# Gate products issued ahead of a block border, and a projection tile cast ahead of the value norm

## What is computed

```python
y_a = chunked_spatial_gating(u, vv, a_spatial_w, a_spatial_b) * silu(a_z)   # vv = layer_norm(gelu(a_v))
gates = sigmoid(g.reshape(bn, s, 3, D_MODEL) + gate_b)                       # g is a slice of h @ w_in
merged = (gates[:, :, 0] * (y_a @ proj_a)
          + gates[:, :, 1] * (y_b @ proj_b)
          + gates[:, :, 2] * (y_m @ proj_m))
x = x + merged @ w_out
```

## Time and profile before

| what | value |
|---|---|
| median of timed runs | 1764.21 us |
| profiled execution | 1767.3 us |
| its span, first to last instruction | 1765.6 us |
| PE busy | 1727.1 us (98%) |
| DVE, ACT, POOL busy | 52%, 37%, 14% |
| mean granted TensorE clock | 0.995 |

### The profile page before, as it was taken

How to read it: one execution, slowest core, us unless ns; L and a number is a source line. 1 busy time by engine, 2 the same in 40 slices (tenths; PEclk the granted TensorE clock), 3 DMA queues, 4 the chain that set the end, 5 groups by cost and what they waited for, 6 DMA issues and landing times.

```text
span 1765.6 us, 22322 instructions
## 1 busy us (share of the span) xinstructions
PE 1727.1 (98%) x8731; PEld 1398.5 (79%) x8731; DVE 915.1 (52%) x1528; ACT 653.4 (37%) x1225; POOL 247.0 (14%) x412
## 2 busy tenths in 40 slices
PE   7999999999999999999999999999999999999998
PEld 5788887778888887778888788888787777777786
DVE  5158868664326753763223322467142555657764
ACT  5234338512324432852112111323213363434731
POOL 3012210288801100000000000490000000000000
PEclk9999999999999999999999999999999999999999
DMA  4121110346232200311111211333613111001132
GB/s 144 55 71 48 36 36 2 118 148 194 77 122 72 60 25 13 93 30 48 54 54 40 84 45 30 108 131 99 129 36 99 37 37 37 25 25 48 38 131 107
DMA packets 148340, 122.93 MB, mean 70 GB/s; under 512 B 10556, under 2 KB 133899, under 8 KB 147595
## 3 DMA queue, kind: packets, MB, share of 16 engines
q1 hardware_dynamic: 148234, 121.49, 22.8%
HBM read 108.21 MB, written 13.26 MB: 69 GB/s over the span
## 4 chain that ended last, share of the span: by engine, by line
PE 53%; DVE 3%; ACT 1%; issue 1%; DMA 1%; SPq 0%; DVEq 0%; ACTq 0%
PE psum L93 29%; PE psum L278 8%; PE psum L81 7%; PE psum L2707 2%; PE psum L2738 2%; PE psum L2721 1%; PE psum L1720 1%; DMA w_raw<-w_in 1%; PE psum L945 0%; PE psum L931 0%; DVE h2T L2340 0%; PE psum L2503 0%; PE psum L2524 0%; PE psum L920 0%; SPq L196 0%
## 5 line engine op out<-in xcount | busy, mean ns | idle before, releaser
L93 PE MATMUL psum<-hT,w_parts 128*128 128x512 f32 x3360 | 796.7, 393 | 7.1 <-PEq L61 3.4
L93 PEld LDWEIGHTS psum<-hT,w_parts 128*128 128x128 f32 x3360 | 629.6, 189 | 144.9 <-issue 9.0
L221 DVE TENSOR_TENSOR w_parts<-w_raw,w_parts 128x1024 fp32r<-128x1024 f32 x88 | 111.6, 1268 | 371.4 <-ACT w_parts L210 371.4
L93 PE MATMUL psum<-h2T,w_parts 128*128 128x512 f32 x1248 | 298.9, 396 | 2.9 <-ACT ssm_u L330 2.9
L93 PEld LDWEIGHTS psum<-h2T,w_parts 128*128 128x128 f32 x1248 | 231.9, 189 | 52.0 <-issue 5.0
L1514 ACT ACTIVATE gate<-psum,cols 128x512 f32<-128x512 f32 x48 | 33.0, 688 | 283.7 <-PE psum L81 283.7
L81 PE MATMUL psum<-y_high,wp_parts 128*128 128x512 f32 x384 | 128.8, 395 | 0.3 <-DVE ya_low L1572 0.3
L210 ACT CAST w_parts<-w_raw 128x1024 fp32r<-128x1024 f32 x88 | 91.6, 1041 | 33.9 <-DMA w_raw<-w_in 29.2
L81 PEld LDWEIGHTS psum<-y_high,wp_parts 128*128 128x128 f32 x384 | 72.0, 188 | 18.9 <-DVE ya_low L1572 1.6
L278 PE MATMUL psum<-w_parts,y_parts 128*128 128x512 f32 x360 | 82.6, 390 | 0.6 <-DVE w_parts L271 0.6
L403 DVE RECIPROCAL x<-x 128x512 f32<-128x512 f32 x24 | 80.3, 3344 | 0.0
(11 more groups left out here) (377 smaller groups left out, 2267.7 us busy)
## 6 DMA issues: line engine op xcount, KB each, us to landing
w_raw<-w_in SPq DMA_DIRECT2D x188, 256.0 KB, 3.4
middle_a<-ada_w SPq DMA_DIRECT2D x32, 384.0 KB, 3.6
w_raw<-w_out SPq DMA_DIRECT2D x16, 512.0 KB, 3.9
qkT<-x SPq DMA_DIRECT2D x8, 512.0 KB, 7.8
w_raw<-m_w_kv SPq DMA_DIRECT2D x16, 256.0 KB, 3.1
base<-x SPq DMA_DIRECT2D x8, 512.0 KB, 4.1
x_kept<-x_ring SPq DMA_DIRECT2D x8, 512.0 KB, 3.4
base<-x_kept SPq DMA_DIRECT2D x8, 512.0 KB, 3.6
```

The costliest lines, as they stand in the source:

```text
L93: last = pe.matmul(out, lhs(a, k), rhs(b, k), start=(n == 0), stop=(n == len(SLOT) - 1))
L221: dve.tensor_tensor(self.parts[:, u, LO, :, :], self.raw[:, :, :], self.parts[:, u, HI, :, :].bitcast(F32), ALU.subtract).then_inc(self.lo ...
```

## The change

TensorE: the 24 products of slot 0 of the merge run are issued by the middle run, 16 ahead of the last turn and 8 behind it, in `FirstProducts`. The merge run then starts with the products of slot 1, and behind them come the projection of slot 0, then that of slot 1. ScalarE and VectorE: the high and the low part of the first gate tile are made when the second last tile of the middle run is done, not at its end. ScalarE, VectorE and SP: the second projection tile is loaded (behind the first tile's low part) ahead of the norm's three loads, cast as soon as slot 1 is done and ahead of the second square root and Gelu, and split ahead of the norm's last steps; `work` now comes ahead of `spatial` in the list.

```diff
@@ Dense.tensor
-            if slot.h == 0:
+            if slot.h == 0 and not (s == 0 and self.opened):
                 pe.wait_ge(self.w.high, 2 * slot.n + 2)
...
+            if s == 0 and self.opened:
+                continue
             slot_part(pe, out, lhs, rhs, range(8))
...
+            if s == 1 and self.opened:
+                tile.extra(pe, self, 0).then_inc(self.made, 1)
+                for work in self.beside:
+                    work.tensor(pe, 0)
             (tile.extra(pe, self, s) or last).then_inc(self.made, 1)
@@ Dense.scalar (Dense.vector likewise with ahead_low)
+            if slot.last and slot.n + 2 == len(self.tiles) and self.ahead:
+                self.ahead.ahead_high(act)
...
-        if self.ahead:
-            self.ahead.ahead_high(act)
+class FirstProducts(Beside):
+    def tensor_end(self, pe):
+        if 0 in self.steps:
+            pe.wait_ge(self.w.high, 2)
+            pe.wait_ge(self.run.free[0], sum(1 for slot in self.run.slots if slot.bank == 0))
+        else:
+            pe.wait_ge(self.w.low, 2)
+        slot_part(pe, bank(self.core, 0, 1), self.w.lhs(0), lambda part, k: self.src[:, part, k, 0:HALF], self.steps)
@@ Projections.sync
-        if s == 0:
+        if s == -1:
             self.load(sp, 1)
@@ Projections.scalar_early
+        if s == 1:
+            act.wait_ge(self.run.made, 2)
+            self.wp_split_high(act, 1)
@@ Projections.vector_early
+        if s == 1:
+            self.wp_split_low(dve, 1)
@@ Projections.scalar (and .vector)
-        if s % 2 and s // 2 + 1 < len(self.tiles):
+        if s % 2 and s // 2 + 1 < len(self.tiles) and s > 1:
@@ merge_run
-    run = Dense(core, w, hT, tiles, [spatial, work])
+    run = Dense(core, w, hT, tiles, [work, spatial])
+    run.opened, work.run = True, run
@@ Middle.prepare
-                               [dilated, self.join, modulation, ssm, mem, turn_mv, attention, self.turn_av],
+                               [dilated, self.join, modulation, ssm, mem, turn_mv, attention, products[0], self.turn_av,
+                                products[1]],
```

More of the change, by code:

```diff
@@ L424, in __init__ @@
     def __init__(self, core, w, src, tiles, beside=(), heads=None, eps=None, ahead=None, crossed=False):
-        self.ahead = ahead
+        self.ahead, self.opened = ahead, False
         self.core, self.w, self.src, self.tiles, self.beside, self.eps = core, w, src, tiles, beside, eps
@@ L554, in vector @@
                 w.split_low(dve, slot.n // 2 + 1, slot.n % 2)
+            if slot.last and slot.n + 2 == len(self.tiles) and self.ahead:
+                self.ahead.ahead_low(dve)
             self.tiles[slot.n].vector(dve, self, s)
@@ L560, in vector @@
         self.tiles[slot.n].vector_last(dve, self, s)
-        if self.ahead:
-            self.ahead.ahead_low(dve)
         for work in self.beside:
@@ L1446, in scalar, with __init__, follow @@
                 act.copy(self.mv[:, t, :], bank(self.core, 6 + t, 1)).then_inc(self.kept, 1)
+class FirstProducts(Beside):
+    def __init__(self, core, w, src, steps):
+        self.core, self.w, self.src, self.steps = core, w, src, steps
+    def follow(self, run):
+        self.run = run
+    def tensor_end(self, pe):
[5 more added lines that the diff above has]
+        slot_part(pe, bank(self.core, 0, 1), self.w.lhs(0), lambda part, k: self.src[:, part, k, 0:HALF], self.steps)
 class TurnTokens(Beside):
@@ L3433, in prepare @@
                               [core.over("mem_pT", [P, 1024], c_at + 8192)[:, :]], (2,), 4, (6,))
+        products = [FirstProducts(core, ahead, self.hT, steps) for steps in (range(16), range(16, 24))]
         self.run = run = Dense(core, w, self.hT, self.tiles,
-                               [dilated, self.join, modulation, ssm, mem, turn_mv, attention, self.turn_av],
+                               [dilated, self.join, modulation, ssm, mem, turn_mv, attention, products[0], self.turn_av,
+                                products[1]],
                                heads=(self.ones, same, roots[:, 2, :], *parts, roots[:, 0:2, :], (4, 5)), eps=self.eps[:, 0:1],
@@ L3438, in prepare @@
         first = run.first_slot(self.first_av)
+        for part in products:
+            part.follow(run)
         turn_mv.follow(run, run.first_slot(self.tiles.index(self.last_mv)))
```

## The result

The kernel after takes 1766.41 us in the median (1764.67 to 1771.37, 22 runs), the kernel before 1764.28 us (22 runs beside it). The ratio is 1.0013, 95% interval 1.0007 to 1.0019: slower by some 2.3 us (0.0013 x 1764.28). The forecast was 1761.1 us and a range up to 1763.4; it had the wrong sign.

What follows compares the result with a forecast made beforehand. TensorE was taken as the bound, busy 1727.1 of 1765.6 us. Removed 0.87 + 3.39 + 1.67, added 1.75 + 0.05 + 1.25: 2.9, taken as 3.1 with the turns' tails; 1764.21 - 3.1 = 1761.1 us, range 1760.2 to 1763.4.

Steps and rivals of the forecast that it cites:

- The end of the middle run: Border: 24 products around the last turn, its 0.87 us wait gone, TensorE's pause 1.75 + 0.05 us instead of 3.39.
- Rival B: TensorE's clock falls again behind the border; slot 1 takes 7.15 us, gain 2.7, time 1761.5 us; chance 0.08.
- The wait for the first gate: Before slot 2 of the merge run, TensorE waits some 1.25 us for ScalarE's first gate to read bank 0.
- R: Time of the release at the border between middle and merge run, forecast 709.3; 706.56 in before.
- one of the forecast's own signs of being wrong: Forecast is wrong if the new TensorE wait of 1.0 to 1.9 us for ScalarE's gate is missing.
- The norm's loads: Merge run: issued 2.8 us later from the border, landing by R + 13.5, covered by 0.8 to 2.8 us.
- rival E: Norm's loads land late and TensorE waits at the first mix, 1 us each past R + 14.3; chance 0.10.
- TensorE is the bound again: Behind the first mix: TensorE's slot takes 8.9 us, ScalarE's work about 7.3 us.
- What follows is again paced by TensorE or starts relative to it: Merge run: a microsecond won or lost at the border goes to the end undiminished.
- The second part: Second projection tile ahead of the norm; left in place it would stop TensorE for up to 3 us at projection 2.
- This edit earns nothing against before: Early second projection tile: no gain against before, but it lets the first edit keep its gain.
- Rival C: Timed runs of before don't pay the 1.67 us of clock at the border; gain 1.45, 1762.8 us; chance 0.12.

Runs made afterwards that it cites:

- hold_first: The kernel after with VectorE's addition of a mixed row (and product with y) ahead of the slot's norm steps: 1761.54 us against 1764.55, ratio 0.9988.
- products_only: The kernel after without the early load, cast and split of the second projection tile: 1767.32 us against 1764.55, ratio 1.0018.
- products_hold: The kernel after without the early second projection tile, with the addition ahead of the norm's steps on VectorE: 1766.53 us against 1764.55, ratio 1.0014.

## Why the prediction was wrong

- **The end of the middle run, right.** The 24 products around the turn, the turn's lost wait, the release at 709.3 (709.54) and the pause of 1.75 + 0.05 (1.85) came as worked out.
- **The clock, wrong but nearly without effect.** Rival B (0.08) came true: half clock behind 1.85 us of pause. It was argued from one pause of 1.82 us at which it stayed at 1.00. The kernels with the first part had a pause of 1.73 to 1.86 us in seven traces; the clock fell in five and stayed in two, one of them at 1.86. The Trainium skill (TensorE: Matmul & The Clock Gate, What's actually happening) was quoted for an effect of idleness; the length of the pause alone doesn't decide it here.
- **The wait for the first gate, right.** The gate came at 719.47 = R + 9.9 (forecast 9.5, the cast at R + 4.6 in place of 4.2), and slot 2 at R + 10.1. In after the slow slot covers the wait, so one of the forecast's own signs of being wrong is there; with the clock up it is 1.4 to 1.5 us, within the 1.0 to 1.9 named. Slot 2's gain was 2.3 us, where 3.1 was forecast. Part of the gap is in the forecast's reading: it took slot 2 of before from the chain of waits (722.02), while the timeline, from which the times after are read, has 721.86. Like with like its gain was 3.0.
- **The norm's loads, right.** There is no wait at the first mix, and GpSimd starts behind them at R + 11.0 (forecast R + 11.5 with free queues). The prediction places their last issue at R + 5.7 in one sum and near R + 6.1 in rival E; it came at R + 5.6.
- **The step that failed** is the end of the part on the norm's loads, "TensorE is the bound again", with which every wait behind the first mix went into the sum as nothing. It compared rates, 8.9 us of TensorE for a slot against 7.3 of ScalarE, and took the faster rate for being in time. But ScalarE's and VectorE's chain starts at the release with a lag, and by these rates it catches up only 1.6 us in a slot. In before TensorE had two slots to do between the release and slot 2, which is the chain's head start; in after it has one. What the working should have held is each instruction with which TensorE waits for this chain in the first slots. The gate and the first norm were there; the addition was missing. The trace of before had it, ending at R + 29.9. By the sum's own times TensorE would reach the mix of row 1 one slot behind the first mix, at R + 16.5 + 8.9 = R + 25.4. That makes a wait of 4.5 us, more than the whole gain of 3.1. The runs showed TensorE at R + 26.1 and a wait of 3.86 us in after, and none in hold_first.
- **"What follows is again paced by TensorE or starts relative to it"** fell with that step. In the first four slots what follows hangs on the release of the border, and the first part moves that release 3 us later.
- **The second part, half right.** It is what keeps the first part's gain (3.2 to 3.3 us of wait at projection 2 without it, "up to 3" forecast). "This edit earns nothing against before" leaves out that alone it costs 6.9 us by the trace and 6.7 by the ratio.
- **Rival C** (the timed runs don't pay the clock) isn't settled. hold_first's timed gain is 0.5 to 3.7 us and its local one 2.6; both C's and the forecast's figure lie in that.

Most of the forecast's gain did exist: hold_first has 2.1 us of it by the ratio and 2.6 by the trace. In after the wait at the mix (3.86) and the clock behind it (some 1.5) turned it into a loss.

What stays open is why the clock falls behind one wait and not behind another of nearly the same length: behind 3.19 us in products_only it fell, behind 3.27 us in products_hold it did not.

## What to carry to other kernels

When an engine gets ahead at a border, list everything that it will wait for until the other engines' chains have caught up, each with its time since the release, and subtract the time at which the engine gets there. An average rate says nothing about the first slots. The wait to look for is one that frees a buffer (here an addition that empties PSUM), queued on a third engine behind a step that needs the slowest chain; moving it forward cost nothing that could be measured and brought out what the larger edit was worth. And try the parts in all their combinations: of the eight kernels here each edit alone was slower than before or the same, and only the three together were faster.

## What the hardware showed

- A wait of TensorE can cost twice, but need not. In products_only 3.19 us of wait were followed by 9 us at a granted clock of 0.50, and the mix in it took 3.76 us. Behind the 3.27 us of products_hold the clock stayed at 1.00, and the mix took 2.18.
- Clearing the same semaphores as one range in place of two shortened the meeting of the engines from 1.86 to 1.73 us. The one clearing took 745 ns and the two 377 and 394, so the clearing itself stayed, at over a third of the meeting.
- The Trainium skill (ScalarE: Activation LUTs, What ACT_TABLE_LOAD costs) was weighed in the prediction. In after too, a load that starts at 717.48 is followed by its activation at 718.78, 1.30 us later; no row here shows the drain.
